# Projections of a two-layer hybrid model: split float32r products replaced by plain float32 products, with a deeper weight ring

## What is computed

```python
h = rms_norm(x); x = x + hybrid_mixer(h)    # gated delta rule (4 heads) + state space scan (8 heads), h @ w_in, @ w_out
h = rms_norm(x); x = x + conv_ffn(h)        # h @ w_up (1024 x 5632), causal conv of 3 taps, silu(a) * b, @ w_down (2816 x 1024)
h = rms_norm(x); x = x + nsa_mixer(h)       # 16 heads: compressed, selected and windowed attention, h @ w_in, @ w_out
h = rms_norm(x); x = x + conv_ffn(h)
out = rms_norm(x)
```

## Time and profile before

| | |
|---|---|
| time, median of 3 runs | 3439.76 us (3438.21 to 3441.07) |
| span of the profiled execution | 3455.9 us |
| PE busy | 3161.6 us, 91% |
| PEld busy | 2612.9 us, 76% |
| DVE, POOL, ACT busy | 1405.7, 1248.5, 938.8 us |
| mean granted TensorE clock | 0.942 of full |
| DMA | 127.5 MB, 37 GB/s |

### The profile page before, as it was taken

One profiled execution on the slowest core, in us unless ns is written; L12 is line 12 of the kernel. 1 busy time (PEld: TensorE's weight loads), 2 busy tenths in 40 slices (PEclk: granted clock), 3 DMA queues, 4 the chain that ended last, 5 costly groups with the idle time before them and its releaser, 6 DMA issues. The chain is left out here.

```text
span 3455.9 us, 41720 instructions
## 1 busy us (share of the span) xinstructions
PE 3161.6 (91%) x16629; PEld 2612.9 (76%) x16629; DVE 1405.7 (41%) x2167; ACT 938.8 (27%) x1447; POOL 1248.5 (36%) x638
## 2 busy tenths in 40 slices
PE   5967889887899999999897899999999899999998
PEld 4747887765778888888685787778878688888887
DVE  3675445353333133133301676655552332232334
ACT  3332223222133011021100454446661231010121
POOL 4325323465454444444642100000004544444442
PEclk8988999998899999999998897879999899999999
DMA  3100001110111111111114000000001111111111
GB/s 132 43 25 1 1 1 31 43 55 25 43 37 48 49 49 46 52 49 44 38 49 122 9 1 1 1 1 1 1 1 37 37 48 46 47 47 50 49 46 70
DMA packets 211543, 127.46 MB, mean 37 GB/s; under 512 B 8904, under 2 KB 208077, under 8 KB 211149
## 3 DMA queue, kind: packets, MB, share of 16 engines
q1 hardware_dynamic: 209600, 125.25, 12.3%
q10 hardware_dynamic: 1805, 0.28, 0.0%
HBM read 112.94 MB, written 8.39 MB: 35 GB/s over the span
## 5 line engine op out<-in xcount | busy, mean ns | idle before, releaser
L403 POOL TENSOR_TENSOR WH<-WR,ONES 128x1024 fp32r<-128x1024 f32 (+1 forms) x194 | 459.8, 2370 | 1355.1 <-PE PS L1312 1280.6
L1312 PE MATMUL PS<-YH,WH 128*128 128x512 f32 x2336 | 738.5, 398 | 63.5 <-POOL YL L428 34.9
L1312 PE MATMUL PS<-YL,WH 128*128 128x512 f32 x2336 | 726.6, 393 | 0.0
L1312 PE MATMUL PS<-YH,WL 128*128 128x512 f32 x2336 | 725.0, 392 | 0.0
L1312 PEld LDWEIGHTS PS<-YH,WH 128*128 128x128 f32 x2336 | 440.8, 190 | 178.5 <-issue 53.9
L1312 PEld LDWEIGHTS PS<-YL,WH 128*128 128x128 f32 x2336 | 444.0, 190 | 93.9
L1312 PEld LDWEIGHTS PS<-YH,WL 128*128 128x128 f32 x2336 | 442.5, 189 | 93.4
L406 POOL TENSOR_TENSOR WL<-WR,WH 128x1024 fp32r<-128x1024 f32 (+1 forms) x194 | 481.1, 2480 | 15.2
L1100 DVE SCALAR_TENSOR_TENSOR X<-PS,PTF,X 128x1023 f32<-128x1023 f32 (+1 forms) x176 | 225.6, 1282 | 573.4 <-ACT X L752 560.7
L752 ACT ACTIVATE X<-PS,PTF 128x1024 f32<-128x1024 f32 x88 | 106.2, 1207 | 840.5 <-PE PS L1312 840.3
L1670 PE MATMUL PS<-X,Z 128*128 128x64 f32 x2112 | 287.4, 287 | 0.0
(11 more groups left out here) (302 smaller groups left out, 3264.2 us busy)
## 6 DMA issues: line engine op xcount, KB each, us to landing
WR<-in_ffn_w_up_dram SPq DMA_DIRECT2D x88, 512.0 KB, 3.8
WR<-in_hy_w_in_dram SPq DMA_DIRECT2D x28, 512.0 KB, 3.8
WR<-in_ffn_w_down_dram SPq DMA_DIRECT2D x32, 448.0 KB, 3.6
WR<-in_ffn_w_down_dram SPq DMA_DIRECT2D x16, 512.0 KB, 3.7
WR<-in_nsa_w_in_dram SPq DMA_DIRECT2D x14, 512.0 KB, 3.7
Z<-in_x_dram SPq DMA_DIRECT2D x8, 512.0 KB, 7.5
xt_scratch<-H SPq DMA_DIRECT2D x1, 4096.0 KB, 12.1
H<-xt_scratch SPq DMA_DIRECT2D x1, 4096.0 KB, 12.3
```

The costliest lines, as they stand in the source:

```text
L403: pool.tensor_tensor(WH[:, slot, 0:k, :], WR[:, slot, 0:k, :], ONES[:, :].unsqueeze(1).broadcast_to([P, k, P]), ALU.mult).then_inc(w_hi, 1)
L1312: ins = pe.matmul(PS[:, 2 * slot + a, :], w[:, slot, i, :], y[:, i, a * HALF:(a + 1) * HALF], start=(i == 0 and w is WH and y is hi), stop ...
```

## The change

All projections are done with plain float32 operands: no WH, WL, YH, YL, MH, ML. POOL's splits and subtractions, ACT's rounding copies and DVE's remainders go. `norm_apply` writes Y (the first 8 tiles of Z) directly and without the wait for POOL. U_HOUT reads its inputs where they lie in X. The turned attention output is copied into Y by ACT for even tiles and DVE for odd ones. WR becomes a ring of six slots, reused when `gemm_done` says that PE has finished the unit that read it. The feed-forward's whole inner layer is kept (`hidden`: 16 tiles of X, 6 of Z), so there are 44 up units and 8 down units of 22 k tiles per layer, 162 units in all, and the loops are written out. The recurrences take the upper half of Z as scratch, so H is neither stored nor reloaded.

```diff
-        WR = sb("WR", [P, 2, MT, P])
-        WH = sb("WH", [P, 2, MT, P], f32r)
-        WL = sb("WL", [P, 2, MT, P], f32r)
+        Y, SC = Z[:, 0:MT, :], Z[:, MT:2 * MT, :]
+        HT = SC.rearrange("p m (a n) -> p (m a) n", a=2)
+        WR = sb("WR", [P, RING, MT, P])
...
+        def hidden(k):
+            return X[:, k, :] if k < 16 else Z[:, MT + k - 16, :]
...
-            def load(n, slot, src):
-                if not isinstance(n, int) or n >= 2:
-                    sp.wait_ge(w_split, n - 1)
-                sp.dma_start(WR[:, slot, 0:src.shape[1], :], src).then_inc(w_loaded[slot], 16)
+            def load(n, src):
+                for b in range(-(-src.shape[1] // MT)):
+                    at = first_load[n] + b
+                    if at >= RING:
+                        sp.wait_ge(gemm_done, unit_of_load[at - RING] + 1)
+                    part = src[:, b * MT:min((b + 1) * MT, src.shape[1]), :]
+                    sp.dma_start(WR[:, at % RING, 0:part.shape[1], :], part).then_inc(w_loaded[at % RING], 16)
...
-            sp.dma_start(xt_scratch, HF).then_inc(spilled, 16)
...
-            sp.dma_start(HF, xt_scratch).then_inc(restored, 16)
...
-            def split(n, slot, k, loads):
-            def y_lower(r, y0):
-            def norm_upper(r):
...
                 for m in range(MT):
-                    if m >= 2:
-                        dve.wait_ge(y_ready, y0 + m - 1)
-                    dve.scalar_tensor_tensor(out=X[:, 17 + m % 2, :], in0=H[:, m, :], scalar=PTF[:, wcol + m:wcol + m + 1],
-                                             in1=PSF[:, 4 * HALF:6 * HALF], op0=ALU.mult, op1=ALU.mult).then_inc(yf_ready, 1)
+                    dve.scalar_tensor_tensor(out=Y[:, m, :], in0=H[:, m, :], scalar=PTF[:, wcol + m:wcol + m + 1],
+                                             in1=PSF[:, 4 * HALF:6 * HALF], op0=ALU.mult, op1=ALU.mult).then_inc(y_ready, 1)
...
-                        dve.tensor_tensor(X[:, 16, :], X[:, 16, :], X[:, 17, :], ALU.mult).then_inc(f_mid, 1)
-                        dve.wait_ge(f_hi, j + (pairs + 1))
-                        dve.tensor_tensor(MLF[:, bass.ds(j * SEQ, SEQ)], X[:, 16, :], MHF[:, bass.ds(j * SEQ, SEQ)].bitcast(f32),
-                                          ALU.subtract).then_inc(f_lo, 1)
+                    dve.tensor_tensor(hidden(j), X[:, 16, :], X[:, 17, :], ALU.mult).then_inc(f_mid, 1)
...
-            def unit(n, slot, k, hi, lo, first_of=None, last_of=None):
-                pe.wait_ge(w_split, n + 1)
-                    for w, y in ((WH, hi), (WH, lo), (WL, hi)):
-                        for a in range(2):
-                            ins = pe.matmul(PS[:, 2 * slot + a, :], w[:, slot, i, :], y[:, i, a * HALF:(a + 1) * HALF],
-                                            start=(i == 0 and w is WH and y is hi), stop=(i == k - 1 and w is WL))
+            def unit(n, moving, ready=None):
+                for i in range(k_tiles(n)):
+                    at = first_load[n] + i // MT
+                    if i % MT == 0:
+                        pe.wait_ge(w_loaded[at % RING], 16 * (at // RING + 1))
+                    if ready is not None:
+                        ready(i)
+                    for a in range(2):
+                        ins = pe.matmul(PS[:, 2 * (n % 2) + a, :], WR[:, at % RING, i % MT, :], moving(i)[:, a * HALF:(a + 1) * HALF],
+                                        start=(i == 0), stop=(i == k_tiles(n) - 1))
...
+            units(U_HOUT, MT, mixed, lambda k: X[:, out_tile(k), :])
...
-                        for w, y in ((GWH, YH), (GWH, YL), (GWL, YH)):
-                            ins = pe.matmul(PS[0:count, 6 + a, :], w[:, i, 0:count], y[:, i, a * HALF:(a + 1) * HALF],
+                        ins = pe.matmul(PS[0:count, 6 + a, :], GWR[:, i, 0:count], Y[:, i, a * HALF:(a + 1) * HALF],
...
-            for m in range(MT):
-                dve.wait_ge(ot_hi, m + 1)
-                dve.tensor_tensor(YL[:, m, :], gemm_ps(m % 2), YH[:, m, :].bitcast(f32), ALU.subtract).then_inc(y_ready2, 1)
+            for m in range(1, MT, 2):
+                dve.wait_ge(ot_ready, m + 1)
+                dve.tensor_copy(Y[:, m, :], gemm_ps(1)).then_inc(y_ready2, 1)
```

More of the change, by code:

```diff
@@ L10, in hybrid_nsa_program @@
                        ffn_w_up, ffn_conv, ffn_conv_bias, ffn_w_down, out):
-    f32, f32r, i32 = mybir.dt.float32, mybir.dt.float32r, mybir.dt.int32
+    f32, i32 = mybir.dt.float32, mybir.dt.int32
     ALU, ACT, AX = mybir.AluOpType, mybir.ActivationFunctionType, mybir.AxisListType
@@ L39, in hybrid_nsa_program, with k_tiles @@
     U_QKV, U_ZA, U_XBC, U_ZB, U_HOUT = 0, 12, 16, 24, 28
-    U_FFN = [36, 126]
-    U_NSA, U_NOUT = 104, 118
+    U_FFN = [36, 110]
+    U_NSA, U_NOUT = 88, 102
+    UNITS = 162
+    U_DOWN = [n + 2 * FT for n in U_FFN]
+    def k_tiles(n):
+        return FT if any(d <= n < d + MT for d in U_DOWN) else MT
+    first_load = [0]
+    for n_ in range(UNITS):
+        first_load.append(first_load[-1] + -(-k_tiles(n_) // MT))
+    unit_of_load = [n_ for n_ in range(UNITS) for _ in range(first_load[n_], first_load[n_ + 1])]
     ctx = ExitStack()
@@ L469, in _ @@
                                            ALU.mult).then_inc(bm_ready, 1)
-            splits(U_ZA + 2, 2)
-            splits(U_XBC, 8)
-            splits(U_ZB, 2)
             for c in range(TT):
@@ L492, in _ @@
                                    ALU.mult).then_inc(hd_ready, 1)
-            splits(U_ZB + 2, 2)
-            splits(U_HOUT, 2)
-            for k in range(MT):
-                pool.wait_ge(os_hi, k + 1)
-                pool.tensor_tensor(YL[:, k, :], X[:, out_tile(k), :], YH[:, k, :].bitcast(f32), ALU.subtract).then_inc(y_ready, 1)
-            splits(U_HOUT + 2, MT - 2)
-            def ffn_splits(l, norm_no, y0):
-                n0 = U_FFN[l]
-                splits(n0, 2)
-                y_lower(norm_no, y0)
-                for first, count in GROUPS:
-                    skip = 1 if first == 0 else 0
-                    loop_splits(n0 + 2 * skip, count - skip, MT)
-                    loop_splits(n0 + 2 * count, MT // 2, count)
-                    n0 += 2 * count + MT
-            ffn_splits(0, 1, 2 * MT)
             for h in range(H16):
@@ L532, in _ @@
                                pattern=[[1, 640]], channel_multiplier=-1).then_inc(wb_ready, 1)
-            splits(U_NOUT, 2)
             pool.wait_ge(h1_ready, 4)
@@ L572, in _ @@
                     at += w
-            splits(U_NOUT + 2, MT - 2)
-            ffn_splits(1, 3, 4 * MT)
         @block.scalar
@@ L765, in _ @@
+            ffn(0, 1, U_HOUT)
+            norm(2, U_DOWN[0])
             act.wait_ge(slopes_ready, 1 + H16)
@@ L810, in _ @@
                     exp_step(p + 1)
-            for m in range(MT):
+            for m in range(0, MT, 2):
                 act.wait_ge(ot_ready, m + 1)
-                act.activation(YH[:, m, :], gemm_ps(m % 2), ACT.Copy).then_inc(ot_hi, 1)
-            ffn(1, 3)
-            norm(4, U_FFN[1] + 60)
+                act.activation(Y[:, m, :], gemm_ps(0), ACT.Copy).then_inc(ot_hi, 1)
+            ffn(1, 3, U_NOUT)
+            norm(4, U_DOWN[1])
             act.wait_ge(rstd_ready, 5)
@@ L1076, in residual @@
                     dve.tensor_tensor(H[:, m, :], H[:, m, :], gemm_ps(n % 2), ALU.add).then_inc(psum_free, 1)
-                    if last and m >= 1:
+                    if m >= 1:
                         norm_sums(r, m - 1)
```

273 lines of the change are left out of this document (87 added, 186 removed).

## The result

The changed kernel takes 3890.72 us (median of four runs, 3884.05 to 3896.77), the kernel before 3440.41 beside it (3438.21 to 3446.66): a ratio of 1.1309, 95% interval 1.1285 to 1.1334. It is slower by 450 us, where 475 was forecast. The profiled execution took 3884.05 us with a span of 3882.3 and a mean granted clock of 0.96.

What follows compares the result with a forecast made beforehand. The prediction took PE's record count times pace to bound the projections. Dearer k tiles (feed-forwards +378, other units +132) and small terms, less savings at norms, U_HOUT and the attention turn, gave +475, 3915 us, range 3885 to 3985.

Steps and rivals of the forecast that it cites:

- The price of a k tile: In all projections: two plain float32 calls, 1.72 us against 1.362 for six float32r records, 0.358 us more per k tile.
- Rival 1: In the projections: dense float32 takes 0.440 us a record, +58 us, 3973 us; 9% together with rival 4.
- Rival 5: In the projections: a call costs one record's time, k tile 0.86 us, -715, about 2660 us; 2%.
- rival 6: In the projections: products stay float32r, one for three, k tile 0.454 us, near 2100 us; 1%.
- Rival 2: In the new projection stretches: the granted clock falls to the span's mean 0.942 instead of 1.00, 4066 us; 2%.
- rival 3: In the 104 written-out units: loops starve PE or DVE of instructions, up to 4015 us; 4%.
- rival 4: At the first units: the savings fail because a weight or another wait holds them, +44, 3959 us; 9% with rival 1.
- q, k, v: First projection stage: longer units partly hide behind a 16.35 us loop of ACT and DVE, so +6 us, not 35.
- Norms: Ahead of both feed-forwards and U_NSA: the first unit ends sooner after the norm, 9.3 us three times, -28 us.
- the splits at 0: POOL's weight splits, with spill, reload, rounding, remainders and ring: removing them worth 0, as PE never waits on a split.
- U_ZB and U_HOUT: State space output stages: longer units, less 12 us for U_HOUT's earlier first unit; +22 us in the stage table.
- U_ZA and U_XBC: Projections between delta rule and state scan: every unit charged 0.358 us more per k tile, +34 us.

Runs made afterwards that it cites:

- e3: The changed kernel with each matmul call cut to 256 columns, four calls a k tile: 3894.57 us.
- e5: The changed kernel with a ring of four and GpSimd's split work put back, unused, from the first layer's out units to the second layer's second unit: 3896.45 us.
- e10: The kernel before with GpSimd's split of the second unit after three norms held until VectorE's adds of squares are done: 3430.39 us, ratio 0.9970.
- e1: The kernel before once more, without any edit, for a second trace: 3435.84 us.
- e6: The changed kernel with a ring of three weight slots instead of six: 3984.25 us.

## Why the prediction was right, and where it was off

**The price of a k tile** held to 0.003 us: 1.717 (0.4292 a record in the unbroken stretches) for 1.72 from four records of the sums of squares. That carried the forecast: 1056 k tiles of the feed-forwards were forecast at +359 with the norms' saving and came to +357. Rival 1 had 0.440 a record; e3 shows why it failed: what a float32r record takes above its columns does not come with plain float32. Rival 5 (a call costs one record) and rival 6 are out with the 6080 records at 0.43. Rival 2, a lower clock, is out with the clock of 1.00; rival 3 with the unbroken piece of 2112 records, since a written-out loop starved nothing; rival 4, because the savings came, and more. (The time that rival 5 gives was summed wrongly: 3440 - 715 - 35 is 2690 us, not 2660.) Of the signs that the prediction names, one went against it: late in the q, k, v stage the reads follow PE.

**Norms.** From the first apply on, the saving was as forecast: the first tap of U_NSA follows the apply by 17.0 us for 23.5, which with 2.9 us for the longer unit is 9.4; 9.3 was taken. The step that fell short was the one that put the splits at 0, because PE never waits on one. They did cost something, not by making PE wait but by slowing VectorE's adds at the norm, 3.1 us three times. It could have been read off the trace: the two adds in the kernel before and the splits beside them,

```profile
926.95 2.36 POOL L403 TENSOR_TENSOR WH<-WR,ONES 128x1024 fp32r<-128x1024 f32 x1 [5.13 <-PE PS L1312]
928.05 5.62 DVE L840 TENSOR_TENSOR X<-X 128x1024 f32<-128x1024 f32 x2
...
929.38 3.20 POOL L406 TENSOR_TENSOR WL<-WR,WH 128x1024 fp32r<-128x1024 f32 x1
```

while other products of the same shape in it take 1.23 us. For the scaled tiles of U_HOUT I had named just this ("slowed by POOL's traffic, which goes") and did not ask where else the two engines meet. e5 and e10 show it from both sides.

**U_ZB and U_HOUT**, +15 for +22. The step that failed is the same one, the splits at 0. In the kernel before all four products with the gate took 2.48 us beside a split, as this one did:

```profile
778.66 2.48 DVE L1057 TENSOR_TENSOR X<-X 128x1024 f32<-128x1024 f32 x1 [16.83 <-ACT X L726]
```

In the changed kernel they take 1.23 us. From the first SiLU to the fourth it went from 59.3 us to 63.7, where three longer units alone would be +8.6: 4.2 of the 7 us that are missing. The other 3 lie between the fourth SiLU and the first residual add. The fourth product has a part in them; the rest is U_HOUT's first unit, for which I had taken 15.9 us from its start to the add, and which needs 13.9. In e5, which slowed only the last two products, they cost 3.6 us.

**q, k, v**, -3 for +6. The step that failed is "From there the period is 16.35 us", which lets the loop of root, reciprocal and taps begin with the sixth read. The loop's first product in the kernel before and in the changed one:

```profile
120.57 2.34 DVE L893 TENSOR_TENSOR X<-X,H 128x1024 f32<-128x1024 f32 x1
```
```profile
119.01 1.23 DVE L794 TENSOR_TENSOR X<-X,Z 128x1024 f32<-128x1024 f32 x1
```

From the second product on they start 16.34 us apart in both kernels, and 15.19 after the fifth. So the loop runs as before, and the stage ends earlier or later by as much as the loop begins so; and it begins with the fourth unit's taps (104.27 us before, 102.72 after). By the forecast's own numbers that would have been +1.7 us and not +6: some 4 of the 9 us. Another 3.3 are the first unit, whose read came at 61.5 us where I had taken 64.7. Its apply was 2.1 us earlier, much of it from VectorE's adds ahead of it: three of them took 1.98, 2.03 and 1.36 us beside GpSimd and take 1.23 now. The first product above gives 1.1 us, and 0.4 lie in the gate columns at the end. ScalarE's reads kept PE's 15.45 us all the while, because the loop needs some units to eat its slack of 4.9 us and there were too few: 2.7 us of it went. A slower stage does not take over at once; how many rounds it has to catch up in is part of the sum.

**U_ZA and U_XBC**, +23 for +34. I charged twelve units at 2.9 us and did not look whether all of them were PE's. PE's waits in the kernel before, from 545 to 606 us:

```profile
PE PS L1312 <- DVE X L1008: 6.6, 2, 4.6
```

U_ZA's roots were 14.0, 16.1 and 14.0 us apart, held by that chain, and became 15.45 each: +2 for three units at 8.6; and the second unit of U_XBC came 17.9 us behind the first and now comes 13.7. The longer records filled time that had been lost to waits: 11 us. In the changed kernel the same list is empty for this stretch. A part of those waits was GpSimd's again. Of the four products of that chain in the kernel before, two took 1.23 us, and the two that PE's waits end with took 3.37 and 3.24, this one beside a split:

```profile
557.80 3.37 DVE L1008 TENSOR_TENSOR X<-X 128x1024 f32<-128x1024 f32 x1
```
```profile
560.17 3.23 POOL L406 TENSOR_TENSOR WL<-WR,WH 128x1024 fp32r<-128x1024 f32 x1
```

That is some 4 of the 6.6 us of waiting. Behind the two waits 17 records start 0.42 to 0.43 us apart instead of 0.23, another 3.4 us, which the changed kernel does not have either.

**Attention** is the same work; 4 us less in these two traces is within the clock's scatter (e1). It is also why 49 us missed in the span are 24 in the time: I took 16 us off for the profiled execution of before, whose span lay that far above its median, and the median of after lies 8 us above its own profiled span.

**The ring of six** was costed at nothing, and e5 (four: nothing) and e6 (three: +89) show the point from which a smaller one would cost: a down unit has three loads.

## What to carry to other kernels

Count TensorE's records and their pace before touching anything else: where PE is busy the whole time, work taken from other engines is worth nothing unless it runs beside a step that PE waits for. Here a product split by hand into three was cheaper than the plain float32 that replaced it, and one product alone gave back its records only once the chain of the other engines was shorter and had a second scratch buffer. Where another engine is on the path for a moment, as at a norm, ask who else works in SBUF in that moment, and hold it back if its result isn't due.

## What the runs showed of the hardware

- A tensor_tensor of VectorE on 128x1024 float32 with both inputs in SBUF took 1.22 to 1.23 us with GpSimd idle (all 95 of the changed kernel) and 2.0 to 3.4 when one of GpSimd lay beside it for nearly all of its time (29 in the kernel before); one that reads PSUM for one of its inputs took 1.21 to 1.23 in both cases. GpSimd's own went from 2.34 up to 3.3 us.
- Starts of records in unbroken stretches: float32r, 512 columns, 0.2267 us, whether or not the weights change; plain float32, two records a call, 0.4292 at 512 columns and about 0.216 at 256.
- Gaps of 4.4 to 5.1 us on TensorE (e6) were each followed by three to six records at half the clock, 2 us lost. The same instructions of the attention took from 654.5 to 671.5 us in two executions, with a granted clock of 0.87 and 0.82 in their first 390 us.
